# The sixth weight slot's request placed behind the first gather, and two shared half products placed behind the second unit

## What is computed

```python
def _moe_ffn(h, w_router, router_bias, w_gate, w_up, w_down, sh_gate, sh_up, sh_down):
    scores = jax.nn.sigmoid(jnp.einsum('bld,de->ble', h, w_router).astype(f32))
    ...                                   # 4 of 8 groups, then 8 of the experts left, for each token
    w = ROUTED_SCALE * w / jnp.sum(w, axis=-1, keepdims=True)
    ...
    def routed_row(args):
        hr, gr = args
        act = jax.nn.silu(jnp.einsum('ld,edf->lef', hr, w_gate)) * jnp.einsum('ld,edf->lef', hr, w_up)
        return jnp.einsum('lef,efd->ld', act * gr[..., None], w_down)
    ...
    shared = jnp.einsum('blf,fd->bld', jax.nn.silu(h @ sh_gate) * (h @ sh_up), sh_down)
    return routed + shared
```

## Time and profile before

| | us |
|---|---|
| runs of the kernel before (3), median | 1609.82 |
| lowest and highest of them | 1605.01 and 1611.59 |
| the profiled execution | 1615.54 |
| its span between first and last instruction | 1613.8 |
| share of the span in which TensorE has a matmul in flight | 91% |
| data moved | 512.46 MB, mean 318 GB/s |
| granted TensorE clock, mean | 0.947 |

### The profile page before, as it was taken

How to read it: one execution, slowest core, us unless ns; L and a number is a source line. 1 busy time by engine, 2 the same in 40 slices (tenths; PEclk the granted TensorE clock), 3 DMA queues, 4 the chain that set the end, 5 groups by cost and what they waited for, 6 DMA issues and landing times. The chain is left out here.

```text
span 1613.8 us, 24656 instructions
## 1 busy us (share of the span) xinstructions
PE 1461.5 (91%) x9414; PEld 864.6 (54%) x9414; DVE 691.3 (43%) x1471; ACT 355.4 (22%) x744; POOL 249.7 (15%) x323
## 2 busy tenths in 40 slices
PE   8999888999898999897999877987999997979996
PEld 6788668887544444353545466863434342424442
DVE  3889747631533343342434258043233332323323
ACT  3766454220410111110111020132011111111111
POOL 5779525200100000000000000001000000000000
PEclk9999999799899999898999978987999998989999
DMA  7679361039389999999999881395999999999994
GB/s 271 208 189 258 129 162 55 2 132 367 142 339 419 423 423 422 425 422 424 420 422 423 365 301 72 129 384 188 363 423 425 422 425 423 423 423 420 426 422 192
DMA packets 101490, 512.46 MB, mean 318 GB/s; under 512 B 36836, under 2 KB 42020, under 8 KB 66300
## 3 DMA queue, kind: packets, MB, share of 16 engines
q1 hardware_dynamic: 91548, 481.81, 75.3%
q0 software_dynamic: 9824, 29.05, 4.9%
HBM read 508.92 MB, written 17.10 MB: 326 GB/s over the span
## 5 line engine op out<-in xcount | busy, mean ns | idle before, releaser
L1986 DVE TENSOR_TENSOR e_ac<-e_sl,banks 128x256 f32<-128x256 f32 x54 | 22.7, 421 | 408.5 <-ACT e_sl L1895 408.5
L1774 PE MATMUL banks<-upper,e_xgT 128*64 128x512 f32 (+1 forms) x864 | 195.5, 612 | 1.3 <-issue 1.1
L304 PE MATMUL banks<-hT,dense_ring 128*128 128x272 f32 x768 | 184.9, 399 | 5.3 <-DMA dense_ring<-in_w_in 5.3
L1381 POOL DMA_INDIRECT x_xg<-rows_dram,x_idx x54 | 53.6, 993 | 848.6 <-DVE x_idx L1373 842.2
L1774 PE MATMUL banks<-dense_ring,e_xgT 128*64 128x512 f32 (+1 forms) x320 | 149.5, 623 | 38.3 <-issue 37.2
L304 PEld LDWEIGHTS banks<-hT,dense_ring 128*128 128x128 f32 x768 | 147.5, 193 | 39.3 <-DMA dense_ring<-in_w_in 5.3
L1774 PE MATMUL banks<-experts,e_xgT 128*64 128x512 f32 (+1 forms) x704 | 153.4, 608 | 0.9 <-issue 0.9
L1774 PEld LDWEIGHTS banks<-dense_ring,e_xgT 128*64 128x64 f32 (+1 forms) x320 | 41.1, 131 | 134.5 <-issue 132.5
L1895 ACT ACTIVATE e_sl<-banks 128x256 f32<-128x256 f32 x54 | 20.8, 385 | 402.4 <-PE banks L1774 402.4
L1792 PE MATMUL banks<-x_sg,route_consts 128*128 128x272 f32 x432 | 104.5, 394 | 2.8 <-ACT route_consts L1910 1.4
L1774 PEld LDWEIGHTS banks<-upper,e_xgT 128*64 128x64 f32 (+1 forms) x864 | 65.1, 132 | 74.4 <-issue 74.4
(11 more groups left out here) (453 smaller groups left out, 2179.0 us busy)
## 6 DMA issues: line engine op xcount, KB each, us to landing
upper<-in_moe_gate_up SPq DMA_DIRECT2D x54, 2048.0 KB, 25.2
experts<-in_moe_gate_up SPq DMA_DIRECT2D x44, 2048.0 KB, 26.9
upper<-in_moe_down SPq DMA_DIRECT2D x44, 1024.0 KB, 25.2
experts<-in_moe_down SPq DMA_DIRECT2D x44, 1024.0 KB, 26.2
dense_ring<-in_moe_down SPq DMA_DIRECT2D x40, 1024.0 KB, 25.0
dense_ring<-in_moe_gate_up SPq DMA_DIRECT2D x20, 2048.0 KB, 15.0
dense_ring<-in_w_in SPq DMA_DIRECT2D x47, 512.0 KB, 4.6
x_gate_up<-in_moe_gate_up SPq DMA_DIRECT2D x10, 2048.0 KB, 19.2
```

Of the source, the lines that this page charges most:

```text
L304: mm = pe.matmul(ps[g % 4][:, 0:T], slot[:, n % SLOTS_IN, c, :], hT[:, c, :], start=(c == 0), stop=(c == DC - 1))
L1381: pool.indirect_dma_start(out=ex["xg"][:, i % 2, :], out_offset=None, in_=mem["rows_dram"], in_offset=bass.IndirectOffsetOnAxis(ap=ex["idx ...
L1774: mm = pe.matmul(gub[e * n:(e + 1) * n, :], xgT[:, i % 2, c, e * n:(e + 1) * n], gate_up_weights(mem, j)[:, c, :], start=(c == 0), stop=(c ...
L1986: dve.tensor_tensor(ac[:], sl[:], gub[:, FF:], ALU.mult).then_inc(mul, 1)
```

## The change

Three edits; nothing of the arithmetic changes, only when requests and half products come.

1. `norm_and_route`, both layers: SP waits for the first gather's rows before it requests expert 5.
2. Layer 0: two half products (the gate halves) stay in `norm_and_route`, and the two of up go behind `turn_act(1)`, as `FC` is 2. With them go VectorE's two multiplications `shared_gate`.
3. Layer 0: expert 4's gate and up weights are no longer requested at the start of `experts`, but as in layer 1: behind those of experts 8 and 9, after a wait on `sh_gu`.

```diff
 def halves_ahead(layer):
-    return 1 if layer == DEPTH - 1 else 2 * FC
+    return 1 if layer == DEPTH - 1 else FC
...
                 sp.wait_ge(ordered, 1)
+                sp.wait_ge(ex["gathered"][0], 16)
                 load_expert(sp, k, mem, layer, RING - 1)
...
-                if not last:
-                    load_gate_up(sp, k, mem, layer, expert_at(sp, mem, FIXED), FIXED)
                 for i, stream in enumerate(UNITS):
                     following = [j + RING for j in stream if j + RING < E]
                     if following:
                         sp.wait_ge(gu, i + 1)
                     for n, j in enumerate(following):
                         load_gate_up(sp, k, mem, layer, expert_at(sp, mem, j), j)
-                        if i == 1 and n == 1 and last:
+                        if i == 1 and n == 1:
                             sp.wait_ge(ex["sh_gu"], 2 * FC)
                             load_gate_up(sp, k, mem, layer, expert_at(sp, mem, FIXED), FIXED)
```

## The result

| | median of runs, us | against before, 95% interval |
|---|---|---|
| before | 1607.96 (10 runs, 1601.8 to 1611.59) | |
| with the change | 1616.76 (10 runs, 1615.87 to 1622.0) | 1.0057 [1.0042, 1.0072] |
| with the change, measured again on another chip | 1617.80 (6 runs) | 1.0054 [1.0033, 1.0074] |

The change costs 9 us (0.57% of 1608), 7 to 12 by the interval. The forecast was +2.1 us with a range of 1605 to 1618. The time, 1616.8, is inside the range, but it lies just beyond the 0.5% that I had called the limit of what can be told, and the size is four times the forecast one. (The forecast was put on the median of the first three runs of before, 1609.82; with all ten that median is 1607.96.) The two profiled spans hardly differ: 1613.8 us before, 1614.9 now. So the first question is why the profiles say +1.1 and the runs +9.

A forecast was written before the change was run, and what follows sets the result against it. A full DMA queue bounds each layer's experts, so only the point where it becomes and stays full counts. Layer 0 +4.2 and layer 1 -2.1 give +2.1 us on 1609.82, so 1611.9 us; range 1605 to 1618.

The forecast's parts named there:

- three signs of being wrong: No pause before layer 0's unit 2, a layer 1 gather of 6 us or more, or layer 0 ending earlier.
- rival B: Layer 1: gather slow for another reason than expert 5's load, SP's wait adds 3.7 us in series; 1617.7 us, chance 0.10.
- Layer 0, until unit 2: Layer 0's experts: first transposes at 439.3, units 0 and 1 7.45 us earlier, nothing of it left at unit 2.
- Layer 0, the queue: Expert 4's weights, last in the queue, land at 483.0; TensorE waits 3.3 us, low clock costs 1.7; layer loses 4.2.
- Layer 1: Entry of layer 1's experts: with SP's wait the gather takes 3.6 us, transposes start at 1108.4, 2.1 us gained.
- A: Layer 0: expert 4's weights land within some 8.4 us of request, unit 2 starts as before; 1606.3 us, chance 0.16.
- C: Layer 0: the 7.45 us are kept, for instance if moved half products cost less; 1600.3 us, chance 0.04.
- D: Layer 0: gather unseen before 436 or block ends later, units 0 and 1 gain less; under 2 us, within forecast's 0.70.

The follow-up runs named there:

- e1: Kernel before plus only the wait for the first gather ahead of expert 5's request, both layers; median 1611.78 against 1608.62 us, ratio 1.0014.
- e6: Kernel before, but layer 1's slot 5 weights (a fixed expert's) are requested just as the first gather is issued, without waiting for the order; ratio 1.0018.

## Why the prediction was right, and where its size was not

The direction, the range and layer 0's mechanism held, and none of the three signs of being wrong appeared. The forecast of no difference that can be told did not hold: 8.8 us are just above the 0.5% that I had set, and ten runs of each tell them from nothing. That the time fell in the range is in part luck. 1616.8 lies nearer to rival B's 1617.7 than to the forecast's 1611.9; the range reached up to 1618 for part of B's sake and for the scatter of the medians, and not because I had doubted the term that failed. And the median that I counted from was 1.9 us above that of all ten runs, which hid a part of the error.

**Layer 0, until unit 2: right.** First transposes 439.39 for 439.3; SyncE's wait covered by ScalarE (SyncE done at 436.1, ScalarE at 438.3); nothing of the 7.4 us left at unit 2.

**Layer 0, the queue: right in every link, low by 0.6 to 1.3 us in size.** Slot 4 landed at 483.7 (forecast 483.0, bounds 481.6 to 484.3); the pause was 4.1 us (3.3), since TensorE was ready at 479.5; the low clock cost 2.4 us (1.7, upper end 2.5): 9.40 against 7.0. Expert 10's weights were requested at 493.9 (492.5) and landed at 501.5 (500.9), 4.8 us later than before. At the layer's end the two profiles differ by 4.75; over three profiles of before and two of the change it is 474.2 to 479.7, 5.5. The forecast had 4.2. Expert 4's load stood behind those of 8 and 9 and did not overtake them: as the last in the queue it took 12.5 to 13.4 us, against 7.6 to 8.4 for a load that met an empty one. The Trainium skill (DMA: Bandwidth & Descriptors, section on queues, rings and completion order) states that each DMA engine takes one queue's descriptors in ring order, though a later one may finish first; the trace agrees with the order.

**Layer 1: the step that failed, a term with the wrong sign.** The prediction said that the transposes would start at 1108.4 "instead of 1110.51", a gain of 2.1 us. The new side of that was nearly right: order to transposes 6.8 us, where the forecast's 1108.4 is 7.7 behind the order. The old side was not: 9.8 us was taken as what the kernel before does, from one execution, although the same gather in layer 0 took 3.6 and the requests lay 0.75 us apart. I named the difference (0.75 us against 2.1), and did not ask how often the two requests lie so close; nor did I read the second gather of layer 0, which by the same trace took 9.8 us at 0.73. In the other five profiles of kernels unchanged there it is 3.9 to 4.4. So the term is not -2.1 but +2.9 us against most runs; and TensorE's longer pause (5.2 us against 2.3) adds about 1: from the first transposes to the end the two changed profiles, e1 and the losing one of before took 503.1 to 503.4 us and e6, with the longest pause but one (8.0), 502.9, the others at most 502.5. Behind the longer pause the clock stays low for longer: over the six us from the first transposes the granted clock was 0.60 on average in the changed profile, 0.72 in the second one of before. Together +3.8 for a run that wins, -3.1 for one that loses. With one loser in six this is +2.7, with layer 0's 5.5 it is **+8.2**, and 9 was measured (7 to 12). The other stages are left out of this sum, as if they evened out over many runs; that is not shown. What the shares of winners and losers are in unprofiled runs can't be seen; one in six is a count of six.

**Why the two profiles showed only +1.1.** By stages, the changed one less the one of before: start to layer 0's router -2.6, the router to the order +2.6, layer 0's experts +4.7, the next mixer +0.8, layer 1's router -1.2, order to transposes -3.1, the rest -0.2. The start, layer 0's router and the next mixer are code that the change leaves alone, and over the thirteen profiles they range over 7.6, 2.7 and 4.4 us. That they nearly cancel in this one pair (-0.4 with layer 1's router) is luck; the lost race is what hides most of the 9 us. A hint stood in the table ahead of the prediction: the profiled execution lay 5.7 us above the median and 4 above the highest of the ten runs, and I had carried these 5.7 us along as a constant. It was no more than a hint, as the second profile of before took 1615.7 and had won the race; it was late elsewhere.

**Rival B** named the right place, SyncE's wait for the gather in series, with +3.7 us, but for the wrong reason. I had it decide by a slow gather; it costs when the gather is fast, because then the block's start, which needs SyncE's two requests, is what comes last. **A** fell (slot 4 took 12.5 us, not 8.4), **C** fell (no product of the moved halves was cheaper: 7.50 us for 7.49), and so did **D** (the units moved by the 7.4 us forecast).

## What to carry to other kernels

- A profile is one execution. Where a term rests on a wait for a transfer, look at how close the two competing requests lie, at every place of the trace where the pair comes, and profile the kernel again: 0.75 us apart lost 6 us, 1.3 us apart 0.5, 1.5 us apart nothing.
- Where the DMA queue is the bound, count the DMA engines' idle time, not TensorE's waits. A request that has to wait for compute should stand as early in the queue as its wait allows without holding up others: as last of 10 MB it cost 5.5 us; ahead of the others, with SyncE held up at the wait, 3.1; right behind experts 6 and 7, with what it waits for moved forward too, nothing.
- A wait placed in a block that all engines have to end is paid by all of them, with everything queued behind it, unless another engine ends later still (layer 0 here). The same wait at the start of the next block cost nothing.

## What the runs showed of the hardware

- A gather of up to 128 rows took 3.4 to 4.6 us from issue to landing when a 2 MB load from another queue was requested 1.28 us or more after its issue (40 gathers), and 9.2 to 11.5 us when that was requested 0.75 us or less after it, or ahead (11 gathers). Nothing was measured between 0.75 and 1.28 us. So some 0.5 us in the order of requests decide over 5; how the load holds the gather up isn't shown. The Trainium skill (DMA: Bandwidth & Descriptors, section on queues, rings and completion order) has each DMA engine go round between its queues a packet at a time. The rows agree in that a gather beside a load takes longer than alone; they don't show the turns.
- After a pause of 4.12 us TensorE's granted clock was 0.50 (1.2 GHz) for about 5 us, over the first part of the next 64 records, which took 9.40 us in place of 7.0.
- Runs of one kernel scattered by 6 to 19 us (0.4 to 1.2%). Stages that no edit touches moved between profiles: layer 0 from the router's start to the order took 30.4, 32.1 or 33.1 us, in all thirteen profiles and nothing between, and each of the three came up once in the three profiles of before. I did not look into the cause.
